# A two-layer trunk on one core: the attention gate in the output weights, the residual first in the accumulators, the overflow round behind the regular product

## The chip, the core and the metric

The kernel runs on one core of one Trainium2 chip. The metric is the device time of one execution in microseconds (us); the number for the kernel before is the median of 3 executions. The engines are TensorE (PE in the profile, its weight loads PEld), VectorE (DVE), ScalarE (ACT), GpSimd (POOL) and SyncE (SP), which here only issues transfers.

## The reference, cut to what matters

256 tokens of 1024 values pass through two layers, all in f32. Each is an attention, a residual with LayerNorm, a mixture of experts, and again a residual with LayerNorm.

```python
for l in range(2):
    sh_a, sc_a, g_a, sh_f, sc_f, g_f = split(silu(c) @ ada_w[l] + ada_b[l], 6)
    h = x * (1 + sc_a) + sh_a
    if l == 0:                     # 16 heads of 64, causal, with a forget gate
        q, k, v, f = h @ fox_w_in
        cum = cumsum(log_sigmoid(f + b_f))
        o = softmax(q k^T / 8 + cum_i - cum_j) v
    else:                          # 8 heads, two score maps each, value width 128
        k1, k2, v = (x * (1 + kv_sc) + kv_sh) @ kv_w
        q1, q2 = h @ diff_w_q
        o = (softmax(q1 k1^T / 8 + alibi) - lam * softmax(q2 k2^T / 8 + alibi)) v
        o = o * rsqrt(mean(o^2) + eps) * g * (1 - lam_init)
    x = layer_norm(alpha * x + (1 + g_a) * (o @ w_o))
    h = x * (1 + sc_f) + sh_f
    gates = grouped_top2(softmax(h @ router_w))      # 2 of 16 experts, from one of 4 groups
    m = sum(gates[e] * ((silu(h @ w_gate[e]) * (h @ w_up[e])) @ w_down[e]) for e in range(16))
    x = layer_norm(alpha * x + (1 + g_f) * m)
```

## The kernel before

**Weights.** 304 MB have to come from HBM. All large weights are cut into pieces of 2 MB, which pass through a ring of six slots. SP loads them in one fixed order; `spent` waits until the consumer of a slot has raised `used`, and `landed` makes a consumer wait for the transfer. A piece holds [1024, 512] of a weight (or [512, 1024] of a down weight).

**Modulation.** The 28 pieces of `ada_w` and `kv_ada_w` form seven groups of four, and not all are left to TensorE. For groups 1, 2, 5 and 6 VectorE multiplies the rows by their values of silu(c): `weigh` (L380 the first, L382 the seven others of a piece) sums the eight k slices of a piece into `acc`; `share(g, q)` is a quarter of a group, so one piece, `mod_sum(g)` lets TensorE add over the partitions (L1355), `mod_rows` adds the bias, `turn_mod` (L1389) turns shift and scale, `spread_gate` (L1397) with L863 spreads a gate row over the partitions into `gbc`. Group 4 goes through TensorE, as `mod_product(4)` (L1338), inside the route of layer 0.

**Layer 0's attention.** The stream is turned, scaled and shifted (`hT`). TensorE then projects keys, the forget gate's 16 columns (L1721, twice 8 columns for each of 8 k slices), values, and queries (`turned_units` L1430 and 1443, `natural_units` L1459). `forget_gate` on ScalarE (L679 to 681) and VectorE (L921 to 925) makes log-sigmoid and its running sum over 256 tokens. Then come 8 steps of one pair of heads each, with 3 more to drain the pipeline: scores, softmax (`soft`), probabilities out and turned (L1492), values, `fox_norm`, `pair_out`. TensorE puts one query unit in each step.

**Output and norm.** `out_part` (L1539) is the output projection, 64 products of 128x512 in layer 0 and 1 together, 32 each. `norm_sums` multiplies each half row block in PSUM by the gate (L992), adds alpha x (L993) and takes statistics (L995); `norm_stats` (L998) and GpSimd's `inv_std` (L548) finish them and L1006 normalises. `gained` on GpSimd (L555 multiply, L556 add, twice) makes the next residual x out of the normalised rows.

**Route.** `turn_stream` turns the normalised rows, `route` computes the router's logits, counts, and the position of each token for its expert; VectorE ranks (L1079 and after) and builds pick matrices (L1114, L1115); `gather` (L1597) fetches the tokens by product with them. `zeroed` (L1590) sets the four accumulator banks to zero with a product by zeros.

**Experts.** 16 experts are taken in 8 pairs. For expert j of a pair `gate_up` (L1615, L1616) makes gate and up for up to CAP = 64 tokens (GpSimd's L574 and L583 provide these windows), L1681 and L1688 turn them, `down` (L1626, L1627) follows, L1162 multiplies by the token's gate, and `add_back` (L1633) adds the 128 rows of a pair to the four accumulator banks by product with a put matrix; it runs one pair later. An expert with over 64 tokens has an `overflow` round: the same chain for the rest, with transposes L1650 and its own add-back. Here layer 0 has one such expert (10) and layer 1 two (11 and 14). The round of expert j stands ahead of expert j's regular product, and `gate_up` frees the two slots of j at its end. At the end of the layer `identa` (alpha on the diagonal) times x is added to the accumulators (L1703), then the last pair's add-back, and the second norm.

**Layer 1's attention.** Keys and values are shared projections of the stream, the query as before. It has 8 steps, one of one head with two score maps each; `diff_norm`, `head_out` and `heads_turned` follow, and output products (`out_part`) fill TensorE's places from step 4 on.

## Time and profile before

| | |
|---|---|
| runs of the kernel | 965.51, 965.51, 964.03 us; median 965.51 us |
| profiled execution | 970.29 us, span 968.6 us |
| mean granted TensorE clock | 0.965 |
| busy TensorE | 890.8 us (92%), 3754 instructions |
| busy weight load | 411.2 us (42%) |
| busy VectorE | 353.6 us (37%), 915 instructions |
| busy ScalarE | 170.6 us (18%) |
| busy GpSimd | 69.4 us (7%) |
| moved by DMA | 303.88 MB, mean 314 GB/s |

A busy share is the time in which an engine works on an instruction, over the span from the first to the last one. The weight load overlaps the products. The granted clock says at which of its two speeds TensorE was allowed to run: 1.0 is 2.4 GHz, 0.5 is 1.2 GHz. A matrix product's time is modelled from the trace, so a busy TensorE isn't necessarily one at its peak.

### The profile page before, as it was taken

To read this page: it belongs to the slowest core of one execution; us is meant where nothing else is said; L and a number is where in the kernel's file an instruction comes from. 1 tells how busy PE (TensorE), PEld (TensorE's weight loads), DVE (VectorE), ACT (ScalarE), POOL (GpSimd) and SP (SyncE) were. 2 spreads that over 40 slices of the span, in tenths; PEclk is the share of its full clock that TensorE was granted. 3 is DMA by queue.
4 is the path that set the end of the run, shared out by engine and by line. 5 is a ranking of instruction groups with operands and counts; after the bars stand their busy time and mean duration, and the time that the engine had idled before them with its cause. 6 is when DMAs were issued, how large, how long until landed. Compare 5 with 4: busy or idle time off the path is not lost.

```text
span 968.6 us, 11410 instructions
## 1 busy us (share of the span) xinstructions
PE 890.8 (92%) x3754; PEld 411.2 (42%) x3755; DVE 353.6 (37%) x915; ACT 170.6 (18%) x374; POOL 69.4 (7%) x110
## 2 busy tenths in 40 slices
PE   7899899999999897999989979889999989889895
PEld 3674674443333332233367458434333333233332
DVE  1286744472221122122259574347222212212215
ACT  1010242012111112011111025401211111111210
POOL 1000000003100000000040000200410000000000
PEclk9899999999999998699989989899999999999998
DMA  9999772848999999099984986212199999949901
GB/s 361 427 408 376 312 304 87 353 177 347 415 430 428 427 430 427 34 417 427 426 354 143 432 359 261 88 51 123 34 431 432 424 431 425 430 189 431 424 32 43
DMA packets 23360, 303.88 MB, mean 314 GB/s; under 512 B 2721, under 2 KB 3233, under 8 KB 5281
## 3 DMA queue, kind: packets, MB, share of 16 engines
q1 hardware_dynamic: 22752, 303.14, 75.2%
q8 instruction: 18, 0.29, 0.1%
q10 hardware_dynamic: 576, 0.34, 0.1%
q14 instruction: 14, 0.11, 0.0%
HBM read 302.42 MB, written 1.05 MB: 313 GB/s over the span
## 4 chain that ended last, share of the span: by engine, by line
PE 81%; DVE 9%; DMA 4%; issue 3%; ACT 1%; POOL 1%; SPq 0%; POOLq 0%; DVEq 0%; ACTq 0%
PE ps L1615 24%; PE ps L1626 12%; PE ps L1633 7%; PE ps L1430 6%; PE ps L1539 5%; PE ps L1443 4%; PE ps L1459 4%; DVE acc L382 3%; PE ps L1597 3%; DMA ring<-in_moe_w_up_dram 2%; DMA ring<-in_moe_w_down_dram 2%; PE ps L1362 1%; PE ps L1338 1%; PE ps L1590 1%; PE ps L1681 1%
## 5 line engine op out<-in xcount | busy, mean ns | idle before, releaser
L1615 PE MATMUL ps<-ring,hT 128*64 128x512 f32 x560 | 256.2, 609 | 17.5 <-issue 10.6
L1616 PE MATMUL ps<-ring,hT 128*64 128x512 f32 x560 | 256.6, 610 | 0.0
L1615 PEld LDWEIGHTS ps<-ring,hT 128*64 128x64 f32 x560 | 75.7, 140 | 177.3 <-issue 177.3
L1626 PE MATMUL ps<-ring,arena 128*64 128x512 f32 x280 | 130.4, 609 | 9.3 <-DMA ring<-in_moe_w_down_dram 5.9
L1627 PE MATMUL ps<-ring,arena 128*64 128x512 f32 x280 | 130.4, 609 | 0.0
L1153 DVE TENSOR_TENSOR arena<-arena,ps 128x256 f32<-128x256 f32 x32 | 13.5, 421 | 250.2 <-ACT arena L746 141.8
L382 DVE SCALAR_TENSOR_TENSOR acc<-ring,csig,acc 128x512 f32<-128x512 f32 x112 | 84.2, 752 | 4.0
L1616 PEld LDWEIGHTS ps<-ring,hT 128*64 128x64 f32 x560 | 75.7, 140 | 0.0
L1626 PEld LDWEIGHTS ps<-ring,arena 128*64 128x64 f32 x280 | 36.1, 139 | 77.4 <-issue 69.2
L1633 PE MATMUL ps<-arena 128*128 128x512 f32 x144 | 66.4, 604 | 0.0
L1162 DVE TENSOR_TENSOR arena<-ps,gbc 64x512 f32<-64x512 f32 x70 | 48.0, 686 | 48.1 <-PE ps L1627 47.0
L1430 PE MATMUL ps<-hT,ring 128*128 128x256 f32 x256 | 60.6, 402 | 3.0 <-ACT hT L631 3.0
L1430 PEld LDWEIGHTS ps<-hT,ring 128*128 128x128 f32 x256 | 51.9, 204 | 11.4 <-ACT hT L631 3.5
L1443 PE MATMUL ps<-ring,hT 128*128 128x512 f32 x128 | 55.8, 594 | 0.0
L583 POOL COPY hT<-arena 128x512 f32 x32 | 19.6, 615 | 432.3 <-PE ps L1616 341.2
L742 ACT ACTIVATE arena<-ps 128x512 f32<-128x512 f32 x16 | 9.6, 598 | 197.5 <-PE ps L1616 197.5
L1633 PEld LDWEIGHTS ps<-arena 128*128 128x128 f32 x144 | 26.0, 189 | 39.8 <-issue 39.8
L1443 PEld LDWEIGHTS ps<-ring,hT 128*128 128x128 f32 x128 | 24.2, 190 | 30.5 <-issue 30.4
L1627 PEld LDWEIGHTS ps<-ring,arena 128*64 128x64 f32 x280 | 36.1, 139 | 0.0
L1539 PE MATMUL ps<-ring,hT 128*128 128x512 f32 x64 | 30.6, 626 | 3.2 <-ACT hT L713 3.2
L1459 PE MATMUL ps<-h,ring 128*128 128x256 f32 x128 | 30.1, 389 | 0.5 <-ACT arena L673 0.5
L1459 PE MATMUL ps<-hT,ring 128*128 128x256 f32 x128 | 29.7, 385 | 0.5 <-ACT arena L673 0.5
(253 smaller groups left out, 905.2 us busy)
## 6 DMA issues: line engine op xcount, KB each, us to landing
ring<-in_moe_w_gate_dram SPq DMA_DIRECT2D x32, 2048.0 KB, 13.9
ring<-in_moe_w_up_dram SPq DMA_DIRECT2D x32, 2048.0 KB, 17.3
ring<-in_moe_w_down_dram SPq DMA_DIRECT2D x32, 2048.0 KB, 16.7
ring<-in_ada_w_dram SPq DMA_DIRECT2D x24, 2048.0 KB, 14.4
ring<-in_fox_w_in_dram SPq DMA_DIRECT2D x6, 2048.0 KB, 9.1
ring<-in_kv_ada_w_dram SPq DMA_DIRECT2D x4, 2048.0 KB, 12.1
ring<-in_kv_w_dram SPq DMA_DIRECT2D x4, 2048.0 KB, 20.5
ring<-in_fox_w_o_dram SPq DMA_DIRECT2D x2, 2048.0 KB, 13.2
```

The lines of the kernel that those rows point to most:

```text
L382: ins = alu.scalar_tensor_tensor(out=dst, in0=w[:, k, :], scalar=csig[:, k:k + 1], in1=dst, op0=ALU.mult, op1=ALU.add)
L1162: d.tensor_tensor(out[lo:lo + CAP, half], ps[part_, bank, :], gbc[part_, 1, half], ALU.mult).then_inc(done, 1)
L1430: mm = t.matmul(ps[:, u % 4, 0:S], wcols(piece)[:, k, cc * P:(cc + 1) * P], src[:, k, :], start=(k == 0), stop=(k == KC - 1))
L1443: mm = t.matmul(ps[:, u % 4, :], hT[:, k, b * P:(b + 1) * P], wcols(piece)[:, k, :], start=(k == 0), stop=(k == KC - 1))
L1459: mm = t.matmul(ps[:, 7, 0:S], wcols(n)[:, k, (c % 4) * P:(c % 4 + 1) * P], src[:, k, :], start=(k == 0), stop=(k == KC - 1))
L1539: mm = t.matmul(ps[:, 2 * b + s_, :], oT[l][:, k, b * P:(b + 1) * P], wcols(n)[:, k, :], start=(k == 0), stop=(k == KC - 1))
L1597: return t.matmul(ps[:, gather_bank(k), :], h[:, b, k * P:(k + 1) * P], pick[:, b, :], start=(b == 0), stop=(b == NB - 1))
L1615: mg = t.matmul(ps[0:CAP, bank, :], lhs(k), wcols(ng)[:, k, :], start=(k == 0), stop=(k == KC - 1))
L1616: mu = t.matmul(ps[CAP:P, bank, :], lhs(k), wcols(nu)[:, k, :], start=(k == 0), stop=(k == KC - 1))
L1626: t.matmul(ps[0:CAP, bank, :], lhs(f), wdown(n)[:, f, 0:512], start=(f == 0), stop=(f == 3))
L1627: mm = t.matmul(ps[CAP:P, bank, :], lhs(f), wdown(n)[:, f, 512:D], start=(f == 0), stop=(f == 3))
L1633: mm = t.matmul(ps[:, 2 * b + q, :], lhs(b), yy(q), start=False, stop=True, skip_group_check=True)
```

## The change

The gate `1 + g_a` of the attention is no longer applied to the product in PSUM: `gate_weights` multiplies the output weights' columns by it, in the ring's slots, on VectorE, during the steps of the attention, so `norm_sums` has one operation less in norms 0 and 2, and TensorE waits on `wo_r` where it waited on the transfer. Alpha x is put into the four banks during the route by `residual` (one block ahead of the counts, the other behind the gather), takes over the zeroing of the banks, and the add at the end of the layer goes; `gained` moves from behind the first pair to right behind the norm, block 1 first. In the expert loop the overflow round of expert j stands behind its regular product, on TensorE, ScalarE and VectorE. The slots of expert 0 are freed after one and two k slices of expert 1's product, those of expert 1 within the add-back.

The forget gate's product now goes four k slices side by side into four strips of 32 rows (`wf` has 32 columns per slice), and a second product with `fsum` adds the strips; that one stands behind the first two value units, and VectorE's part stands one unit later. The last quarter of group 2 is summed in steps 0 and 1 of layer 0's attention in place of ahead of them, and mod_sum(2) is issued in step 1; likewise the last quarter of group 6 in steps 0 to 2 of layer 1's attention, with mod_sum(6) behind query 3. In layer 1 `diff_norm(p - 1)` now stands ahead of `soft`. Of the route's filler, mod_product(4) takes the place of zeroing products in the norm and in the route, and turn_mod(4) moves up. The output products of layer 1 are regrouped around the turned heads. Some small tiles move from the arena into `fold`.

```diff
@@ -551,7 +556,7 @@
                 pool.wait_ge(xn_r, 4 * (norm + 1))
-                for b in range(NB):
+                for b in (1, 0):
@@ -593,12 +598,12 @@
                 pair(0, xs_ev)
-                gained(2 * l)
...
             number_slots(0)
+            gained(0)
@@ -675,7 +681,8 @@
             def forget_gate():
                 unit_filled(act, GATE_UNIT)
-                act.wait_ge(small_in, 16 * SMALL)
+                a.activation(fT, ps[:, 0, 0:S], ACT.Copy).then_inc(f_in, 1)
+                act.wait_ge(f_mm, 1)
@@ -740,10 +747,10 @@
                     a.activation(gu[:, 0, :], ps[:, 4, :], ACT.Copy).then_inc(gu_ev[0], 1)
-                    overflow(i, 1)
                     act.wait_ge(tg_mm[0], q + 1)
...
                     a.activation(sg[:, 0, :, :], gt[:, :, 0:CAP], ACT.Sigmoid).then_inc(sg_r[0], 1)
+                    overflow(i, 1)
                     spent(act, n0 + 3, i)
...
+            def gate_weights(l, s_, q):
+                n = N_WO[l][s_]
+                landed(dve, n)
+                w = wcols(n)[:, 4 * q:4 * q + 4, :]
+                d.tensor_tensor(w, w, gbc[:, 0, 512 * s_:512 * s_ + 512].unsqueeze(1).broadcast_to([P, 4, 512]),
+                                ALU.mult).then_inc(wo_r, 1)
             def diff_norm(hd):
@@ -989,9 +1010,8 @@
                     return
-                link(d.tensor_tensor(h[:, b, half], gbc[:, norm % 2, half], ps[:, 2 * b + s_, :], ALU.mult))
-                link(d.scalar_tensor_tensor(out=xres[:, b, half], in0=xres[:, b, half], scalar=ALPHA, in1=h[:, b, half],
-                                            op0=ALU.mult, op1=ALU.add))
+                link(d.scalar_tensor_tensor(out=xres[:, b, half], in0=xres[:, b, half], scalar=ALPHA,
+                                            in1=ps[:, 2 * b + s_, :], op0=ALU.mult, op1=ALU.add))
@@ -1195,8 +1215,8 @@
                     put_pair(i)
+                    glu(0, q)
                     overflow(i, 1)
-                    glu(0, q)
...
-                    forget_gate()
-                else:
+                if u != GATE_UNIT:
                     unit_out(u, dst, kind)
                 if u == GATE_UNIT + 1:
+                    forget_gate()
                     mod_rows(1)
@@ -1238,9 +1257,9 @@
             share(2, 2)
-            share(2, 3)
-            mod_rows(2)
             for p in range(PAIRS_H + 3):
+                if p == 2:
+                    mod_rows(2)
@@ -1251,10 +1270,16 @@
                     fox_norm(2 * p - 1)
+                if p < 2:
+                    share(2, 3, range(4 * p, 4 * p + 4))
                 if p >= 3:
                     pair_out(p - 3)
+                if p in (5, 6):
+                    gate_weights(0, 0, p - 5)
                 if p == PAIRS_H:
+                    gate_weights(0, 1, 0)
                     mod_rows(3)
+                    gate_weights(0, 1, 1)
             nothing_added()
@@ -1294,25 +1318,30 @@
                 slope = (2.0 ** (-8.0 * (p + 1) / HD))
-                if p == 1:
+                if p == 3:
                     mod_rows(6)
+                if 1 <= p < HD - 1:
+                    diff_norm(p - 1)
                 if p >= 2:
...
                     head_out(p - 4)
-                if p >= 1:
-                    diff_norm(p - 1)
+                if p < 3:
+                    share(6, 3, ((0, 1, 2), (3, 4, 5), (6, 7))[p])
+                elif p < HD - 1:
+                    gate_weights(1, (p - 3) // 2, (p - 3) % 2)
+            diff_norm(HD - 2)
             diff_norm(HD - 1)
             head_out(4)
-            heads_turned(1)
+            heads_turned(1, 7)
@@ -1401,8 +1430,10 @@
                 for b in range(NB):
-                    if b and norm != 1:
-                        zeroed((0, 1, 0, 1))
+                    if b and norm == 0:
+                        mod_product(4, range(0, 2))
+                    if b and norm == 2:
+                        zeroed((0, 1, 0))
...
+            def out_weights(l, count):
+                pe.wait_ge(wo_r, 4 * l + count)
             def scored(G):
...
             def route(l):
                 m = (1, 4)[l]
-                zeroed((2, 3))
+                if l == 0:
+                    mod_product(4, range(2, 4))
+                else:
+                    zeroed((0, 1))
...
                         k = 4 * kk + strip
-                        mm = t.matmul(ps[32 * strip:32 * strip + 32, 0, 0:S], rw[:, k, :], hT[:, k, :],
+                        mm = t.matmul(ps[32 * strip:32 * strip + 32, 2, 0:S], rw[:, k, :], hT[:, k, :],
@@ -1567,10 +1602,10 @@
                 if l == 0:
-                    zeroed((0, 2))
-                    mod_product(4, range(0, 4))
+                    mod_product(4, range(4, KC))
                 else:
-                    zeroed((0, 2, 3, 0, 2, 3))
+                    zeroed((0, 0, 0))
+                residual(l, 1)
@@ -1579,11 +1614,15 @@
                 if l == 0:
-                    mod_product(4, range(4, KC))
+                    turn_mod(4, 5)
                 pe.wait_ge(tot_r, l + 1)
-                zeroed((1,) if l == 0 else (1, 1, 1))
-                if l == 0:
-                    turn_mod(4, 5)
+                zeroed((1, 1, 1))
+            def residual(l, b):
+                pe.wait_ge(x_ready, 2 * NB * l + 2 - b)
+                for q in range(2):
+                    t.matmul(ps[:, 2 * b + q, :], identa[:, :], xres[:, b, q * 512:q * 512 + 512], start=True, stop=True)
@@ -1656,33 +1689,40 @@
                             pe.wait_ge(o_dve, k + 8)
-                            add_back(lambda bb: oputT[0:CAP, bb * P:(bb + 1) * P],
-                                     lambda q: oy[0:CAP, q * 512:q * 512 + 512]).then_inc(o_pe, 1)
+                            for bb in range(NB):
+                                for q in range(2):
+                                    mm = add_back(bb, q, oputT[0:CAP, :], oy[0:CAP, :])
+                            mm.then_inc(o_pe, 1)
                 gather()
+                residual(l, 0)
                 pe.wait_ge(tab, l + 1)
...
                     pe.wait_ge(tp_ev, q + 1)
-                    overflow(i, 0)
                     pe.wait_ge(y_ev[0], (q + 1) * 2)
...
                     pe.wait_ge(xw_r[0], q + 1)
-                    gate_up(0, i, lambda k: xw[:, 0, k, :], 4, range(KC), True)
+                    gate_up(0, lambda k: xw[:, 0, k, :], 4, range(KC))
+                    overflow(i, 0)
                     pe.wait_ge(y_ev[1], (q + 1) * 2)
-                    overflow(i, 1)
                     landed(pe, n0 + 2, i)
...
                     pe.wait_ge(xw_r[1], q + 1)
-                    gate_up(1, i, lambda k: xw[:, 1, k, :], 5, range(4), False)
+                    gate_up(1, lambda k: xw[:, 1, k, :], 5, (0,)).then_inc(used[slot(n0)], 1)
+                    gate_up(1, lambda k: xw[:, 1, k, :], 5, (1,)).then_inc(used[slot(n0 + 1)], 1)
+                    gate_up(1, lambda k: xw[:, 1, k, :], 5, range(2, 4))
                     pe.wait_ge(gu_ev[0], q + 1)
...
                     mm.then_inc(tg_mm[0], 1)
-                    gate_up(1, i, lambda k: xw[:, 1, k, :], 5, range(4, KC), True)
-                    add_back(lambda b: putT[:, b * P:(b + 1) * P],
-                             lambda qq: y[:, qq * 512:qq * 512 + 512]).then_inc(sc_mm, 1)
+                    gate_up(1, lambda k: xw[:, 1, k, :], 5, range(4, KC))
+                    overflow(i, 1)
+                    add_back(0, 0, putT, y).then_inc(used[slot(n0 + 2)], 1)
+                    add_back(0, 1, putT, y).then_inc(used[slot(n0 + 3)], 1)
+                    add_back(1, 0, putT, y)
+                    add_back(1, 1, putT, y).then_inc(sc_mm, 1)
                     pe.wait_ge(gu_ev[1], q + 1)
@@ -1697,17 +1737,12 @@
                     down(1, lambda f: aT[:, 1, f * CAP:(f + 1) * CAP], 5).then_inc(used[slot(n0 + 5)], 1)
-                pe.wait_ge(x_ready, 2 * NB * l + NB)
-                for b in range(NB):
-                    for q in range(2):
-                        t.matmul(ps[:, 2 * b + q, :], identa[:, :], xres[:, b, q * 512:q * 512 + 512],
-                                 start=False, stop=True, skip_group_check=True)
...
                 for b in range(NB):
-                    add_back(lambda b: putT[:, b * P:(b + 1) * P],
-                             lambda qq: y[:, qq * 512:qq * 512 + 512], (b,)).then_inc(sc_mm, 1)
+                    add_back(b, 0, putT, y)
+                    add_back(b, 1, putT, y).then_inc(sc_mm, 1)
@@ -1715,20 +1750,20 @@
             pe.wait_ge(small_in, 16 * SMALL)
-            for k in range(KC):
-                for half in range(2):
-                    lo = 64 * half
-                    mm = t.matmul(ps[lo:lo + PAIRS_H, 0, 0:S], wf[:, k, PAIRS_H * half:PAIRS_H * (half + 1)], hT[:, k, :],
-                                  start=(k == 0), stop=(k == KC - 1))
+            for kk in range(2):
+                for strip in range(4):
+                    mm = t.matmul(ps[32 * strip:32 * strip + 32, 0, 0:S], wf[:, 4 * kk + strip, :], hT[:, 4 * kk + strip, :],
+                                  start=(kk == 0), stop=(kk == 1))
...
             u = natural_units(u + 1, N_V[0][:1])
+            pe.wait_ge(f_in, 1)
+            t.matmul(ps[0:FROWS, 0, 0:S], fsum[:, :], fT, start=True, stop=True).then_inc(f_mm, 1)
...
             query_unit(0, 1, hT)
-            mod_sum(2)
@@ -1819,18 +1857,17 @@
             turn_heads(2)
+            turn_heads(3, 4)
+            spread_gate(3, 5)
...
                 out_part(1, 0, s_, range(4, 6))
-            turn_heads(3)
+            pe.wait_ge(ot_ev[1], 2)
             for s_ in range(2):
-                out_part(1, 1, s_, range(4, 6))
-            turn_mod(6, 4)
-            spread_gate(3, 5)
-            pe.wait_ge(ot_ev[1], 2)
-            for b in range(NB):
-                for s_ in range(2):
-                    out_part(1, b, s_, range(6, KC))
+                out_part(1, 0, s_, range(6, KC))
+            turn_mod(6, 7)
+            for s_ in range(2):
+                out_part(1, 1, s_, range(4, KC))
```

## Rows read from the trace of the kernel before

**Rows 1.** The page's slices: what the DMA queues moved, GB/s, 40 slices of 24.2 us.

```profile
GB/s 361 427 408 376 312 304 87 353 177 347 415 430 428 427 430 427 34 417 427 426 354 143 432 359 261 88 51 123 34 431 432 424 431 425 430 189 431 424 32 43
```

**Rows 2.** The chain of work that ended last: start, us on the chain, what.

```profile
368.11 18.66 DMA ring<-in_moe_w_down_dram
...
418.13 3.63 PE ps L1633 x8
...
482.10 3.63 PE ps L1703 x8
```

**Rows 3.** TensorE's timeline, expert stages: start, us, what, in brackets the wait before.

```profile
372.22 0.61 PE L1615 MATMUL ps<-ring,hT 128*64 128x512 f32 x1 [0.19 <-DMA ring<-in_moe_w_up_dram]
...
849.26 0.65 PE L1650 MATMUL ps<-ident,hT 128*128 128x128 f32 x4 [0.78 <-ACT hT L729]
...
857.02 3.70 PE L1633 MATMUL ps<-arena,fold 64*128 64x512 f32 x8 [1.51 <-DVE arena L1162]
```

**Rows 4.** Windows: length, busy PE, PEld, DVE, ACT, POOL, clock, DMA share, GB/s.

```profile
382.20:406.10 23.90, 17.77 (x38) 5.25 (x40) 2.78 (x8) 0.74 (x1) 0.00 (x0) 0.57 0.30 127
575.20:580.20 5.00, 4.95 (x20) 2.39 (x21) 2.05 (x11) 0.72 (x3) 0.00 (x0) 0.50 0.51 211
```

**Rows 5.** Timeline of layer 1's attention and its norm, TensorE and VectorE.

```profile
575.25 1.94 PE L1355 MATMUL ps<-acc,ones 128*32 128x512 f32 x8 [4.55 <-ACT arena L673]
...
614.11 5.47 PE L1539 MATMUL ps<-ring,hT 128*128 128x512 f32 x8 [2.36 <-ACT hT L713]
...
643.83 7.03 PE L1539 MATMUL ps<-ring,hT 128*128 128x512 f32 x16
...
657.43 0.21 DVE L998 BATCH_NORM_AGGREGATE mv<-bst 128x2 f32<-128x12 f32 x1
```

**Rows 6.** Timeline of layer 0's norm, route and gather.

```profile
181.87 13.90 PE L1539 MATMUL ps<-ring,acc 128*128 128x512 f32 x32
...
198.89 0.21 DVE L998 BATCH_NORM_AGGREGATE mv<-bst 128x2 f32<-128x12 f32 x1
...
200.18 1.15 DVE L1006 TENSOR_SCALAR h<-xres,mv,st 128x512 f32<-128x512 f32 x2 [1.08 <-POOL st L548]
...
207.42 0.19 DVE L1079 TENSOR_TENSOR rt<-rt,st 128x32 f32<-128x32 f32 x1
...
214.99 0.75 DVE L1115 SCALAR_TENSOR_TENSOR arena<-arena,ends 128x512 f32<-128x512 f32 x1
...
217.76 13.90 PE L1597 MATMUL ps<-arena,h 128*128 128x512 f32 x32
```

**Rows 7.** Timeline of layer 0's projections, gate and first scores.

```profile
65.59 3.63 PE L1721 MATMUL ps<-hT,wf 128*8 128x256 f32 x32
...
75.31 0.22 DVE L925 COPY arena<-arena 72x128 f32<-72x128 f32 x1
...
84.96 0.66 PE L1389 MATMUL ps<-ident,mrow 128*128 128x128 f32 x4 [0.81 <-DVE mrow L849]
...
110.85 1.06 PE L1355 MATMUL ps<-acc,ones 128*32 128x512 f32 x8 [2.13 <-DVE acc L382]
...
122.06 0.82 PE L1492 MATMUL ps<-ident,arena 128*128 128x128 f32 x6
```

**Rows 8.** VectorE's groups by line and shape: busy us, mean ns, idle before.

```profile
L382 DVE SCALAR_TENSOR_TENSOR acc<-ring,csig,acc 128x512 f32<-128x512 f32 x112 | 84.2, 752 | 4.0
L1162 DVE TENSOR_TENSOR arena<-ps,gbc 64x512 f32<-64x512 f32 x70 | 48.0, 686 | 48.1 <-PE ps L1627 47.0
L380 DVE TENSOR_SCALAR acc<-ring,csig 128x512 f32<-128x512 f32 x16 | 8.5, 534 | 0.1
L863 DVE SCALAR_TENSOR_TENSOR gbc<-ps,gbc 128x1024 f32<-128x1024 f32 x4 | 4.9, 1225 | 4.7 <-PE ps L1397 4.7
```

**Rows 9.** Timeline of VectorE and GpSimd, 502 to 506.

```profile
502.59 2.35 POOL L556 TENSOR_TENSOR xres<-xres,lnw 128x1024 f32<-128x1024 f32 x1
503.88 1.35 DVE L380 TENSOR_SCALAR acc<-ring,csig 128x512 f32<-128x512 f32 x1
```

106 lines of the change are left out of this document (56 added, 50 removed).

## The prediction

> **What bounds the kernel now.** I read the slices of the page first: the DMA row stands at 425 to 432 GB/s through most of the two expert stages, falls to 34 in the seventeenth slice (387 to 412 us) [rows 1]. Then the chain of work that ended last. In layer 0 it goes through a transfer of a down weight, from 368.11 on for 18.66 us, and reaches the add-back of the same pair at 418.13 only [rows 2]. The timeline places this: pair 5 (of 0 to 7) starts at 372.22 with expert 10's overflow round, which stands ahead of the regular product. Its gate and up product (16 half steps of 0.43) is over at 379.1, its transposes come about 1 us behind, and then TensorE waits for the weight until 386.8 [rows 3]. So transfers set the pace up to pair 5 (six pieces of 2.1 MB at 428 GB/s are 29.4 us, against some 26 us of products), and from there on TensorE does: gate and up slots 0 and 1 stay occupied through the overflow, the queue runs dry, TensorE waits, and its clock is 0.57 on average from 382 to 406 [rows 4].
>
> Outside the experts TensorE sets the time, with three kinds of gaps: sums of VectorE that it waits for (4.55 us at 575.25, 2.36 at 614.11) [rows 5], the norm behind the output products (last product ends at 195.8, statistics at 199.1; in layer 1 at 650.9 and 657.6) [rows 5, 6], and the clock after such gaps: 4.5 us of idleness around 572, then 5.0 us at 0.50, which is 1.2 GHz in place of 2.4 [rows 4, 5].
>
> **The change, part by part** (minus is time gained; the working is done on the profiled run of 970.29 us, whose span is 968.6; the median shown is 965.51).
>
> *Forget gate.* Its 16 products of 8 columns take 3.63 us at 65.59 [rows 7]; for four side by side I take a quarter and 0.2, 1.1, so the value product starts 2.5 us sooner. But the sum over strips is now issued behind the two value units (13.9 us) and everything of the gate stands behind it: it would run at 80.6 to 81.0. From the old product's end (69.2) to the gate's last copy (75.31 + 0.2) are 6.3 us of ScalarE and VectorE [rows 7]. VectorE does them ahead of mod_rows(1), so that copy is over at 81.0 + 6.3 + 0.7 = 88.0, and turn_mod, which ran at 84.96, waits 6 us on TensorE, with the gate rows and the other value units queued behind it, and on VectorE the sums of ada(2) wait behind the gate too: 3.15 later. Taken back: the 2.13 us wait for the last sum ahead of the scores and mod_sum(2) itself (1.06) no longer stand there, 3.2. Net 0. The clock: as after the gap at 572 [rows 4], 5 us at half, +2.5 (bounds 0 and 3.4).
>
> *share(2,3) in steps 0 and 1.* The moved half quarter is four operations of 0.75 to 0.79 us, 3.1 us [rows 8]. In step 1 it begins when VectorE has normalised, 9.3 us after the first scores; it is over 12.4 after them, mod_sum(2) needs it, and with its 1.06 us the transposes start 13.5 after them; now the first scores stand at 111.9 and those transposes at 122.06, 10.2 after them [rows 7]: +3.4 (bounds 0, if the half quarter fitted into VectorE's idle time, and 4.2). Later steps take 6.6 us of TensorE and leave VectorE 2.2 idle; into steps 5, 6 and 8 comes a gate product over 128x2048. By the row of 128x1024 (1.23 us) and that of 128x512 (0.69) one costs 2.3 us [rows 8] (bounds: 2.1 and four of the short ones, 2.8). The 0.1 to 0.2 it sticks out lies behind TensorE's 1.5 us between scores and values: 0. WO1 lands long before step 8.
>
> *Norm 0.* Four products of 0.69 go away. Only those of the last half count, because the last output product ends at 195.8: statistics at 195.8 + 0.2 + two operations 1.44 + 0.24 = 197.7, against 199.1: -1.4 [rows 6].
>
> *Route 0.* mod_product(4) replaces the zeroing products of equal length, and its second half (3.6 us) no longer stands between the counts and the gather, which starts at 217.76 though its first matrix was ready at 215.75: -1.9. The residual products (1.8 us each) fill places where zeroing or a wait stood: 0 while POOL is in time. That is where gained costs: four POOL operations, 2.42 us apart, now run right behind the norm, from 0.1 to 9.75 us after its end at 201.3, alongside VectorE's ranking, whose first operation on two SBUF tiles is at 207.42, 6.1 after it [rows 6]. The trace has one such meeting: L380, whose other 15 take 0.48 us on average (8.5 less 1.35, by 15) [rows 8], took 1.35 while POOL's L556 ran, and ended 0.3 behind it [rows 9]. The same here: L1079 waits for the third operation to end (7.3), L1080 for the fourth (9.75): +3.5 (0 if only L380's kind waits; 9.7 is the bound if each started later). TensorE then has 3.5 us with nothing, so I add 1.7 of clock. The Trainium skill, SBUF — State Buffer, section "SBUF: two separate sides", says that the shared ports are locked for a whole instruction, also against VectorE operations with two SBUF inputs. By that rule the sum stays as it is; without it both layers together would be 10.4 us shorter.
>
> *Experts.* Slots 0 and 1 are freed 0.9 and 1.7 us later, slots 2 and 3 the same. The transfers start that much later once: +0.9. After that four more pieces (19.6 us) are under way whenever slot 0 is freed, so nothing more. Pair 5 of layer 0: regular product 372.2 to 379.1, overflow product to 386.0, transposes at 387.0. A round not held by a transfer goes from transposes to add-back in 7.76 us (849.26 to 857.02) [rows 3]: add-back at 394.8, at full clock over at 398.4, then 7.5 us of expert 11's product, and the regular add-back at 405.9, against 418.13: -12.2. In layer 1 the rounds are expert 11's in pair 5 and one in pair 7; neither waits for its down weight, same work in another order: 0. Tail: 3.63 us of residual at 482.10 go; y needs two products of 0.69 [rows 8] and 0.2, so the last add-back can start at 483.7, not 485.7: -2.0, in each layer.
>
> *Attention 1.* The wait of 4.55 at 575.25 and the slow clock behind it [rows 4, 5] go, since 5.8 us of sums leave the place ahead of the first scores. Followed step by step (share of 2.1, 2.4 and 1.6 us in steps 0 to 2, mod_sum(6) once the query of step 3 is copied), the values of head 0 come 6 us sooner. Diff_norm ahead of soft ends a wait in step 7, 2 us more. VectorE's steps come to 6.0 us with the gate product against TensorE's 5.5 and slip 1.5 in all, so the first output product waits for the last gate product until 604.4, where it waits for the turned heads until 614.11 now: -9.7 so far [rows 5]. Behind it no slow stretch and four moved parts: the last output product ends at 638.2, not 650.9 (27.5 us of products, 32 of 0.86, and 6.3 of transposes, values and gate rows behind 604.4). The norm's first block now runs beside it, and the last statistics are out at 640.8, not 657.6: -16.8 in all. The transposes behind them lose their slow clock too (-1.1). POOL's lock and clock again: +3.5 and +1.7.
>
> Sum: layer 0: +2.5 + 3.4 - 1.4 - 1.9 + 3.5 + 1.7 + 0.9 - 12.2 - 2.0 = -5.5. Layer 1: -16.8 - 1.1 + 3.5 + 1.7 + 0.9 - 2.0 = -13.8. Together -19.3: 951.0 for the profiled run, 946.2 for the median.
>
> **Rivals.** *No lock*: POOL and VectorE pass each other. For it: one meeting is all the trace has, and L380 could have been late for another reason [rows 9]. -10.4 more: 935.8. *VectorE bounds attention 1*: its slips reach TensorE, or the gate product costs its upper bound of 2.8 and POOL's rms is late; half of the 16.8 is lost: 954.6. Against it: 2 us of slack per step now. *The overflow order brings nothing*: something other than the down weight ends that wait. Against it the chain's 18.66 us [rows 2]. 958.4. *Slower*: late slots starve the transfers. If each of the 14 pairs that follow a first one paid the 1.7 us, 24 us, the time would be 970; it turns from gain to loss at 1.4 us a pair. Against it: the queue holds four pieces then.
>
> **Chances.** Forecast 0.47 (its own range 941 to 951), no lock 0.25, VectorE-bound 0.15, overflow order without effect 0.08, starved transfers 0.05. The likeliest is 946; the range 934 to 957 takes in the second and third and leaves out less than 2 in 10. The measurement tells 0.2% (1.9 us) from no change. Faster 0.93, same 0.02, slower 0.05.
>
> **What would show it.** Turn_mod's products at about 88 with a 6 us gap before them and a clock of 0.5 behind it; 2 us of waiting at the moved mod_sum(2); L1079 and L1080 of up to 2.4 us under a POOL operation; no DMA slice under 100 GB/s in layer 0's experts, and pair 5's add-back about 34 us behind its start, where it is 46 now; first output product of layer 1 some 38 us behind the first scores, where it is 48 now. Wrong it would be if a transfer-bound pair took more than 29.4 us, or if the route took as long as before in spite of a waiting rank operation.

## The result, and the profile after

The changed kernel took 956.09 us (median of 6 executions), the kernel before 965.51: ratio 0.987, interval 0.984 to 0.990. Measured again, 955.33 against 967.08: 0.988 (0.984 to 0.992); one execution of the kernel before, 1063.07 us at a mean clock of 0.838, was in a slower state and isn't counted. The time is inside the range (934 to 957), one us below its upper end and 10 us above the forecast of 946: about half of the 19.3 us forecast. The profiled execution took 949.71, close to the 951.0 forecast for it, but it was the fastest of its kernel, and that of before (970.29) one of the slowest of its own. Between the two profiled ones 20.6 us are gone, between the medians 9 to 12.

The page's slices of the kernel after (TensorE's granted clock in tenths, and GB/s) answer to [rows 1]:

```profile
span 948.0 us, 11352 instructions
...
PE 869.6 (92%) x3720; PEld 404.5 (43%) x3721; DVE 370.2 (39%) x918; ACT 168.0 (18%) x373; POOL 69.7 (7%) x110
...
PEclk9999999998999999999989999998999999999998
...
GB/s 359 432 421 428 277 321 90 355 206 326 242 430 428 427 429 429 271 322 431 425 428 143 375 418 338 89 156 22 66 431 429 427 427 430 429 209 428 428 60 44
```

The seventeenth slice holds 271 GB/s in place of 34. The early stage, TensorE and VectorE, answers to [rows 7]:

```profile
62.71 1.07 PE L1755 MATMUL ps<-hT,wf 128*32 128x256 f32 x16
...
82.14 0.48 DVE L934 TENSOR_SCALAR fold<-ps,colb 72x256 f32<-72x256 f32 x1 [9.78 <-ACT fold L688]
...
85.09 1.12 PE L1418 MATMUL ps<-ident,mrow 128*128 128x128 f32 x4 [5.95 <-DVE mrow L862]
...
122.77 1.07 PE L1384 MATMUL ps<-acc,ones 128*32 128x512 f32 x8 [2.27 <-DVE acc L387]
```

Turn_mod's products stand behind a gap of 5.95 us and mod_sum(2) behind 2.27. The window behind the first gap (length, busy PE, PEld, DVE, ACT, POOL, clock, DMA share, GB/s) shows the clock at half for 3.4 us:

```profile
84.50:87.90 3.40, 2.81 (x7) 1.77 (x8) 3.26 (x6) 0.00 (x0) 0.00 (x0) 0.51 1.04 443
```

Layer 0's route, VectorE beside GpSimd, answers to [rows 6]:

```profile
206.21 2.37 POOL L560 TENSOR_TENSOR xres<-h,lnw 128x1024 f32<-128x1024 f32 x1
...
206.44 0.19 DVE L1095 TENSOR_TENSOR rt<-ps,st 128x32 f32<-128x32 f32 x1
206.93 0.19 DVE L1097 TENSOR_REDUCE st<-rt 128x2 f32<-128x32 f32 x1 [0.29 <-ACT rt L725]
207.15 0.17 DVE L1098 RECIPROCAL st<-st 128x2 f32<-128x2 f32 x1
207.35 1.27 DVE L1099 TENSOR_TENSOR rt<-rt,st 128x32 f32<-128x32 f32 x1
208.66 2.42 POOL L561 TENSOR_TENSOR xres<-xres,lnw 128x1024 f32<-128x1024 f32 x1
208.66 0.19 DVE L1100 TENSOR_TENSOR rt<-rt,rb 128x32 f32<-128x32 f32 x1
208.89 2.34 DVE L1072 TENSOR_TENSOR rc<-rt 128x128 f32<-128x128 f32 x1
...
214.80 0.64 PE L1612 MATMUL ps<-rt,before 128*128 128x32 f32 x2 [3.14 <-DVE rt L1111]
```

L1099 (0.19 us in the kernel before) takes 1.27 and ends with GpSimd's operation; the next, L1100, still takes 0.19, and its record begins at the same 208.66 as that of GpSimd's fourth operation; L1072 (0.29 alone) takes 2.34. L1095, which reads PSUM, is not held, nor are L1097 and L1098, which read one SBUF tile each. TensorE waits 3.14 us for the ranks, 4.13 in layer 1, and behind both waits its clock is at half for 6.8 us (layer 0 here: 206 to 226):

```profile
206.00:216.00 10.00, 6.86 (x44) 2.89 (x43) 8.38 (x26) 0.83 (x2) 5.00 (x3) 0.91 0.51 185
216.00:226.00 10.00, 10.00 (x24) 5.13 (x24) 6.51 (x29) 0.00 (x0) 0.00 (x0) 0.75 1.01 429
```

Pair 5 of layer 0, the tail, and layer 1's attention, on TensorE, answer to [rows 2, 3, 5]:

```profile
392.97 0.65 PE L1683 MATMUL ps<-ident,hT 128*128 128x128 f32 x4 [0.78 <-ACT hT L736]
395.57 1.11 PE L1662 MATMUL ps<-ring,fold 128*64 128x512 f32 x1 [1.72 <-DVE fold L1205]
402.16 3.70 PE L1667 MATMUL ps<-arena,fold 64*128 64x512 f32 x8 [1.51 <-DVE arena L1182]
413.54 3.70 PE L1667 MATMUL ps<-arena 128*128 128x512 f32 x8
...
479.84 3.67 PE L1667 MATMUL ps<-arena 128*128 128x512 f32 x8 [1.60 <-DVE arena L1182]
...
575.64 1.06 PE L1384 MATMUL ps<-acc,ones 128*32 128x512 f32 x8 [0.56 <-ACT arena L679]
...
599.09 3.70 PE L1572 MATMUL ps<-ring,hT 128*128 128x512 f32 x8 [1.19 <-DVE ring L986]
...
625.93 7.03 PE L1572 MATMUL ps<-ring,hT 128*128 128x512 f32 x16
```

The 5.88 us wait for the down weight is gone, pair 5 (start 378.29) reaches its add-back 35.3 us later, and 45.8 before. Mod_sum(6) waits 0.56 in place of 4.55, and the last output product ends at 633.0, not 650.9. VectorE's groups (busy us, mean ns | idle before):

```profile
L986 DVE TENSOR_TENSOR ring<-ring,gbc 128x2048 f32<-128x2048 f32 x8 | 18.3, 2283 | 0.0
...
L1072 DVE TENSOR_TENSOR rc<-rt 128x128 f32<-128x128 f32 x2 | 4.7, 2330 | 0.1
L1099 DVE TENSOR_TENSOR rt<-rt,st 128x32 f32<-128x32 f32 x2 | 2.5, 1234 | 0.1
```

### The profile page after: what moved, and what is told of

It is laid out like the page before. It is cut to its first block, busy times and chain, and to the rows that moved or that the text cites. A ratio compares the mean times of both kernels' runs of the same rounds, so it can differ in the third digit from the quotient of the medians.

```text
span 948.0 us, 11352 instructions
## 1 busy us (share of the span) xinstructions
PE 869.6 (92%) x3720; PEld 404.5 (43%) x3721; DVE 370.2 (39%) x918; ACT 168.0 (18%) x373; POOL 69.7 (7%) x110
## 4 chain that ended last, share of the span: by engine, by line
PE 79%; DMA 9%; DVE 7%; issue 2%; ACT 1%; POOL 0%; SPq 0%; DVEq 0%; ACTq 0%
PE ps L1654 23%; PE ps L1662 10%; DMA ring<-in_moe_w_up_dram 8%; PE ps L1667 7%; PE ps L1461 6%; PE ps L1474 6%; PE ps L1490 6%; PE ps L1572 5%; PE ps L1636 3%; PE ps L1718 1%; PE ps L1629 1%; PE ps L1391 1%; DMA ring<-in_ada_w_dram 1%; PE ps L1523 1%; PE ps L1426 1%
## 5 line engine op out<-in xcount | busy, mean ns | idle before, releaser
L1654 PE MATMUL ps<-ring,hT 128*64 128x512 f32 x560 | 251.4, 600 | 17.7 <-DMA ring<-in_moe_w_up_dram 9.3
L1655 PE MATMUL ps<-ring,hT 128*64 128x512 f32 x560 | 251.8, 601 | 0.0
L1663 PE MATMUL ps<-ring,arena 128*64 128x512 f32 x256 | 116.7, 599 | 0.0
L1662 PE MATMUL ps<-ring,arena 128*64 128x512 f32 x256 | 116.7, 598 | 0.0
L1173 DVE TENSOR_TENSOR arena<-arena,ps 128x256 f32<-128x256 f32 x32 | 13.5, 421 | 240.8 <-ACT arena L752 132.1
L1461 PE MATMUL ps<-hT,ring 128*128 128x256 f32 x256 | 58.3, 392 | 3.4 <-issue 1.9
L1662 PEld LDWEIGHTS ps<-ring,arena 128*64 128x64 f32 x256 | 32.4, 136 | 60.1 <-issue 60.1
L1474 PE MATMUL ps<-ring,hT 128*128 128x512 f32 x128 | 55.8, 594 | 0.0
L1474 PEld LDWEIGHTS ps<-ring,hT 128*128 128x128 f32 x128 | 24.2, 190 | 30.5 <-issue 30.4
L1663 PEld LDWEIGHTS ps<-ring,arena 128*64 128x64 f32 x256 | 32.4, 136 | 0.0
L1490 PE MATMUL ps<-hT,ring 128*128 128x256 f32 x128 | 29.7, 385 | 0.5 <-ACT arena L679 0.5
L1572 PE MATMUL ps<-ring,hT 128*128 128x512 f32 x64 | 28.6, 594 | 1.2 <-DVE ring L986 1.2
## 6 DMA issues: line engine op xcount, KB each, us to landing
ring<-in_kv_w_dram SPq DMA_DIRECT2D x4, 2048.0 KB, 19.3
```

What stands on the lines that cost most here:

```text
L1461: mm = t.matmul(ps[:, u % 4, 0:S], wcols(piece)[:, k, cc * P:(cc + 1) * P], src[:, k, :], start=(k == 0), stop=(k == KC - 1))
L1474: mm = t.matmul(ps[:, u % 4, :], hT[:, k, b * P:(b + 1) * P], wcols(piece)[:, k, :], start=(k == 0), stop=(k == KC - 1))
L1490: mm = t.matmul(ps[:, 7, 0:S], wcols(n)[:, k, (c % 4) * P:(c % 4 + 1) * P], src[:, k, :], start=(k == 0), stop=(k == KC - 1))
L1572: mm = t.matmul(ps[:, 2 * b + s_, :], oT[l][:, k, b * P:(b + 1) * P], wcols(n)[:, k, :], start=(k == 0), stop=(k == KC - 1))
L1654: t.matmul(ps[0:CAP, bank, :], lhs(k), wcols(ng)[:, k, :], start=(k == 0), stop=(k == KC - 1))
L1655: mm = t.matmul(ps[CAP:P, bank, :], lhs(k), wcols(nu)[:, k, :], start=(k == 0), stop=(k == KC - 1))
```

## The experiments

Executions of one kernel differ by 2 to 12 us, so each row of this table has, beside the median time, the mean over its executions of span and of granted clock, and the mean of span times clock of each: the span with each us at half clock counted half. "Of before" is the ratio with its interval. The changed kernel stands twice, as first measured and again. The rows were measured at three times, and the kernel before, each time beside them, had medians of 967.1, 968.8 and 968.1 us and 937.6, 937.9 and 939.0 in span times clock: a difference of 1 to 2 us between two rows of the table says little.

| kernel | median us | of before | span | clock | span x clock |
|---|---|---|---|---|---|
| before_again | 968.28 | 1.000 (0.997 to 1.003) | 965.1 | 0.971 | 937.3 |
| before_order | 962.91 | 0.996 (0.994 to 0.999) | 960.9 | 0.975 | 936.7 |
| changed | 956.09 | 0.987 (0.984 to 0.990) | 953.6 | 0.971 | 926.2 |
| again | 955.33 | 0.988 (0.984 to 0.992) | 953.6 | 0.970 | 925.0 |
| old_order | 954.01 | 0.986 (0.982 to 0.989) | 951.8 | 0.973 | 926.3 |
| sum2_first | 953.99 | 0.987 (0.983 to 0.991) | 951.3 | 0.970 | 922.8 |
| sum6_first | 962.12 | 0.994 (0.992 to 0.997) | 960.1 | 0.967 | 928.8 |
| gate_in_norm | 958.11 | 0.991 (0.988 to 0.994) | 956.6 | 0.972 | 929.9 |
| late_x | 950.97 | 0.982 (0.979 to 0.986) | 948.5 | 0.975 | 924.9 |
| gate_later | 946.40 | 0.978 (0.973 to 0.983) | 943.9 | 0.976 | 921.1 |
| fix_both | 939.48 | 0.972 (0.968 to 0.976) | 937.9 | 0.982 | 921.0 |
| fix_old | 938.14 | 0.972 (0.968 to 0.977) | 937.6 | 0.984 | 922.9 |
| fix_three | 936.94 | 0.969 (0.965 to 0.973) | 935.1 | 0.983 | 918.8 |

**Both kernels again.** No edit. For the changed one and the one before:

> The changed kernel unaltered, to see how its executions differ. Its six executions lay between 949.71 and 958.81 us with a mean granted clock of 0.978 down to 0.968, and the profiled one was the fastest. Theory: they do the same work and differ only in how many stretches TensorE runs at 1.2 GHz, so span times clock stays constant (948.0 x 0.978 = 927, 956.9 x 0.968 = 926), and a slower execution shows more half-clock stretches in its records, none at the places that the change made busy. Median 953 to 958, ratio 0.987 to 0.992. Rival: executions differ in waits for transfers; span times clock would then spread by several us, and the TensorE waits in the expert stages would be longer in a slower one.

> The kernel before unaltered. The profiled execution was 970.29 us at clock 0.965 (968.6 x 0.965 = 935), its others had a median of 965.51. By the theory of one constant product, 965.5 goes with a clock of 0.970, and the change is worth 8 to 9 us at equal clock and not the 20.6 between the two profiled executions. Rival: at equal clock the difference is 17 us or more, the clock of before is then 0.975 or more at 965 us. Ratio to before 0.998 to 1.002.

Measured: the first holds. Over the changed kernel's twelve executions the span runs from 948.0 to 956.9 and the clock from 0.978 to 0.966, but span times clock only from 923.0 to 927.1. Before and changed have the same mean clock (0.971 and 0.970 to 0.971) and differ by 11 to 12 us in span times clock, so the gain is work and waits, and none of it clock. My figure of 8 to 9 us at equal clock came from two single executions and was too low; the rival's 17 falls.

**old_order.** In the changed kernel, on TensorE (ScalarE and VectorE likewise):

```diff
                     pe.wait_ge(tp_ev, q + 1)
+                    overflow(i, 0)
                     pe.wait_ge(y_ev[0], (q + 1) * 2)
...
-                    gate_up(0, lambda k: xw[:, 0, k, :], 4, range(KC))
-                    overflow(i, 0)
+                    gate_up(0, lambda k: xw[:, 0, k, :], 4, range(KC), True)
                     pe.wait_ge(y_ev[1], (q + 1) * 2)
+                    overflow(i, 1)
```

> The changed kernel with the overflow rounds ahead of the regular products again, and the gate and up slots freed at the end of their product. The forecast's term: the order was worth 12.2 us in layer 0 against 0.9 for late slots in each layer, so this comes out 10.4 slower than the changed kernel, about 966. The two traces gave 9.2 between pair 5's start and its add-back, so by them +9, and TensorE waits 5 to 6 us for expert 10's down weight again with no transfer from its gate product to pair 6. Rival (the order brings nothing): within 2 us of the changed kernel.

Measured: 954.01 against 955.33, not 9 to 10 slower. The rival holds for the time, though not for the reason that the prediction gave it: the wait for the down weight is back. TensorE's timeline of old_order, and the window over pair 5 up to pair 6, then that of the kernel after and that of before:

```profile
392.94 1.12 PE L1665 MATMUL ps<-ring,fold 128*64 128x512 f32 x1 [5.87 <-DMA ring<-in_moe_w_down_dram]
```

```profile
378.36:430.06 51.70, 43.55 (x176) 15.47 (x178) 9.19 (x23) 8.07 (x10) 1.23 (x2) 0.93 0.68 284
```

```profile
378.20:425.00 46.80, 42.78 (x178) 14.88 (x176) 9.34 (x23) 8.07 (x10) 1.23 (x2) 0.96 0.71 296
```

```profile
372.20:429.60 57.40, 49.23 (x178) 16.77 (x180) 9.21 (x23) 8.08 (x10) 1.23 (x2) 0.82 0.61 256
```

With the same wait the place takes 51.7 us at clock 0.93 and 57.4 at 0.82. Of the 10.6 us between before and after, 5.7 were the clock behind the wait and 4.9 the order, and the order gives 2.0 back: in old_order's and again's traces 138.75 and 140.72 us lie between pair 0's and pair 5's start, as the slots come free later. Before_order, the same edit the other way, has 139.43 where both traces of before have 138.74, and fix_both further down has 139.48 where fix_old has 139.82, so this price is between nothing and 2.0. These are single traces, each with its own stretches at half clock: from pair 5 of layer 1 to the last statistics old_order takes 135.0 us at a clock of 0.95 and again 129.1 at 1.00, and with the corrections it is the other way round (fix_old 129.5, fix_both 133.8).

**before_order.** The kernel before, with the changed kernel's order and slot releases in the expert loop:

```diff
-                    overflow(i, 0)
                     pe.wait_ge(y_ev[0], (q + 1) * 2)
...
-                    gate_up(0, i, lambda k: xw[:, 0, k, :], 4, range(KC), True)
+                    gate_up(0, i, lambda k: xw[:, 0, k, :], 4, range(KC), False)
+                    overflow(i, 0)
                     pe.wait_ge(y_ev[1], (q + 1) * 2)
-                    overflow(i, 1)
...
-                    gate_up(1, i, lambda k: xw[:, 1, k, :], 5, range(4), False)
+                    gate_up(1, i, lambda k: xw[:, 1, k, :], 5, (0,), False).then_inc(used[slot(n0)], 1)
+                    gate_up(1, i, lambda k: xw[:, 1, k, :], 5, (1,), False).then_inc(used[slot(n0 + 1)], 1)
+                    gate_up(1, i, lambda k: xw[:, 1, k, :], 5, range(2, 4), False)
```

> The kernel before with one part of the change: the overflow rounds behind the regular products on TensorE, ScalarE and VectorE, with the slot releases that this needs. Undoing it in the changed kernel cost nothing measurable. New theory: the order saves about 3 us of work in pair 5 of layer 0 and nothing in layer 1, the later slots cost 2 us in each layer before pair 5, and what was large in the trace of before was the slow clock behind the 5.9 us wait (20.4 us at half, 10.2 lost), which isn't there in each execution. So span times clock stays within 2 of before's 937, the time is 0 to 5 us shorter, by as much as the slow stretch in pair 5 goes. The forecast's term of 12.2 less 1.8 asks for 10.4 us shorter, 957.

Measured: 5.9 us faster than the 968.78 beside it (by mean spans 4.6), span times clock the same within 1, clock 0.975 for 0.971. So in this kernel the order is worth some 5 us (the interval allows 1 to 6), all of it clock; in the changed one it is worth nothing that the runs tell (old_order's clock is not lower). Neither is the forecast's 10.4.

**late_x.** Gained behind the route's tables, both residual blocks behind the gather, zero products in the first one's place:

```diff
             number_slots(0)
+            pool.wait_ge(tab, 1)
             gained(0)
...
-                residual(l, 1)
+                zeroed((3, 3, 3, 3))
                 pe.wait_ge(rt_mask, l + 1)
...
                 gather()
+                residual(l, 1)
                 residual(l, 0)
```

> The changed kernel with gained behind VectorE's route tables (GpSimd waits for them) and both residual blocks behind the gather; zero products stand where the first residual block stood. Theory of the port: no VectorE operation of the ranking takes 1.2 or 2.3 us, the counts come 3.1 to 3.5 sooner, TensorE's gap of 3.1 and 4.1 us and the slow clock behind it (1.7) go, and 1.9 us of residual stand behind the gather, partly over the wait for the windows of the first pair: 3 to 5 us a layer, 6 to 9 in all, about 948. Rival (the gap has another cause, or a 1.2 GHz stretch only moves elsewhere): under 3 us in all.

Measured: 4.4 us faster, between the 6 to 9 expected and the rival's "under 3". In span times clock nothing is gained (924.9, again 925.0): the gain is clock. Its timeline of VectorE, GpSimd and TensorE (the two ranking operations are now L1101 and L1074):

```profile
212.66 0.19 DVE L1101 TENSOR_TENSOR rt<-rt,st 128x32 f32<-128x32 f32 x1
213.11 0.29 DVE L1074 TENSOR_TENSOR rc<-rt 128x128 f32<-128x128 f32 x1
...
218.53 0.30 PE L1614 MATMUL ps<-rt,before 128*128 128x32 f32 x2
...
226.51 2.35 POOL L560 TENSOR_TENSOR xres<-h,lnw 128x1024 f32<-128x1024 f32 x1 [20.68 <-DVE tabb L1157]
226.66 2.22 DVE L887 TENSOR_TENSOR modc<-colb 128x8 f32<-128x8 f32 x1
...
236.32 3.60 PE L1627 MATMUL ps<-xres,identa 128*128 128x512 f32 x8
```

Both run at 0.19 and 0.29, TensorE's wait is gone, and the lock has moved with GpSimd to an operation off the path (L887, 2.22 in place of 0.17; it holds up the scaling of the first gathered rows, not of the last). From the last output product to the gather 19.9 us pass in place of 23.25 (again), and 19.6 in place of 25.4 in layer 1, less 1.6 in each for the residual behind the gather: 1.8 and 4.2, 6.0 in these traces. Two things changed together: the ranks come 3.1 us sooner behind the logits, and the zero products fill 1.7 us more than the residual block did (3.7 for 2.0), so that in layer 0 TensorE reaches the counts 1.6 us after the ranks are out (216.93). The 6.8 us at half clock are gone in both layers. Whether a shorter filler would do as well no run shows.

**gate_later.** In VectorE's projections:

```diff
                 if u == GATE_UNIT + 1:
-                    forget_gate()
                     mod_rows(1)
...
                     share(2, 0)
+                    forget_gate()
```

> The changed kernel with VectorE's part of the forget gate moved behind mod_rows(1) and the first quarter of ada(2). Theory: turn_mod waits for VectorE's gate work only, so its 5.95 us gap falls to under 2 and the slow stretch behind it goes; VectorE itself gains only the 3 us that it waited for ScalarE's logarithm, so its last sum comes 3 us sooner and TensorE then waits about 5 at mod_sum(2) where it waits 2.3: 3 us shorter, up to 5 if the clock stays high, 950 to 953. Rival (something else, a transfer, ends the gap): no change.

Measured: 946.40, 8.9 us faster than the changed kernel, more than expected. Its TensorE timeline:

```profile
81.55 0.66 PE L1418 MATMUL ps<-ident,mrow 128*128 128x128 f32 x4 [0.81 <-DVE mrow L862]
...
117.89 1.07 PE L1384 MATMUL ps<-acc,ones 128*32 128x512 f32 x8 [2.28 <-DVE acc L387]
```

The gap is 0.81, and the wait at mod_sum(2) didn't grow; it is 2.28, as in again. My reckoning that the 5 us would turn up there was wrong: VectorE starts the last half quarter when it has done a softmax, so those sums follow TensorE's scores and come earlier with them (mod_sum(2) stands 12.65 us behind the first scores in both). In span times clock it is 4 to 5 us, the rest is clock (0.976). The executions spread from 939.0 to 950.6, so the 8.9 is good to some 4 us.

**sum6_first, sum2_first.** The moved quarters undone, one each, with mod_sum and mod_rows of that group where they stood before:

```diff
             share(6, 2)
+            share(6, 3)
...
-                if p < 3:
-                    share(6, 3, ((0, 1, 2), (3, 4, 5), (6, 7))[p])
```

```diff
             share(2, 2)
+            share(2, 3)
+            mod_rows(2)
             for p in range(PAIRS_H + 3):
...
-                if p < 2:
-                    share(2, 3, range(4 * p, 4 * p + 4))
```

> The changed kernel with the last quarter of group 6 summed ahead of layer 1's first scores again and mod_sum(6) ahead of step 1, as before. The forecast gave 16.8 us to attention 1 and its norm, with this move as the start of it. Theory: the 4 to 5 us wait at mod_sum(6) and 3 us of slow clock come back, the following steps run without the 6.1 us of sums: 5 to 7 us slower in all, 960 to 962. Rival (VectorE bounds the whole phase, wherever the sums stand): under 2 us slower.

> The changed kernel with the last quarter of group 2 summed ahead of the first scores and mod_sum(2) there, as before. The forecast said that moving it costs 3.4 us net of 3.2 taken back. Theory: the 2.3 us wait at mod_sum(2) and its 1.1 us leave step 2, but VectorE's 6.1 us of sums stand ahead of the first scores, where VectorE idles only 7.6 us until its first softmax: TensorE waits there for the last sum by 0 to 3 us. Within 2 us of the changed kernel, 953 to 957. If VectorE's time ahead of the scores were free, 3 us faster.

Measured: 962.12 and 953.99. Their waits at mod_sum, on TensorE:

```profile
572.98 1.94 PE L1383 MATMUL ps<-acc,ones 128*32 128x512 f32 x8 [4.29 <-ACT arena L679]
```

```profile
112.64 1.06 PE L1382 MATMUL ps<-acc,ones 128*32 128x512 f32 x8 [0.57 <-ACT arena L679]
```

In layer 1 the move is worth 6.8 us, 3 in span times clock and the rest clock. In layer 0 it is worth nothing (1.3 us the other way, 2 to 3 in span times clock): there VectorE was in time for the first scores, and the move made the wait. It was in time because TensorE had already lost 5.95 us at turn_mod; in the kernel before, TensorE waited 2.13 us for the same sum [rows 7]. What the place of these sums is worth beside gate_later no run shows.

**gate_in_norm.** No gate_weights (TensorE waits for the transfers of the output weights again), the gate in `norm_sums` again:

```diff
-                link(d.scalar_tensor_tensor(out=xres[:, b, half], in0=xres[:, b, half], scalar=ALPHA,
-                                            in1=ps[:, 2 * b + s_, :], op0=ALU.mult, op1=ALU.add))
+                link(d.tensor_tensor(h[:, b, half], gbc[:, 0, half], ps[:, 2 * b + s_, :], ALU.mult))
+                link(d.scalar_tensor_tensor(out=xres[:, b, half], in0=xres[:, b, half], scalar=ALPHA, in1=h[:, b, half],
+                                            op0=ALU.mult, op1=ALU.add))
```

> The changed kernel with the gate in the norm again (one more product of 0.69 us per half block in norms 0 and 2) and none of the eight products over 128x2048 on the output weights. Forecast: 1.4 us longer at each of the two norms; the 1.2 us for which layer 1's first output product waits for the last weight product go, and step times of VectorE fall. Theory: 1 to 2 us slower, 956 to 958. Rival (the weight products hold up the attention steps by more than they save): as fast or faster.

Measured: 958.11, 2.8 slower than again (4 to 5 in span times clock). The statistics of norm 0 come 3.3 us behind the last output product, in the changed kernel 1.7 (199.03 less 197.33). So the 18.3 us of weight products that VectorE took on (L986) do lie beside other work, all but the 1.2 us for which layer 1's first output product waits for the last of them.

**The corrections together.** Fix_both is late_x and gate_later; fix_old adds old_order; fix_three adds to fix_both, on TensorE (VectorE's mod_rows(2) likewise; mod_sum(2) stands at the head of the loop's step 2 in the changed kernel, not in step 1 as the text on the change has it):

```diff
-                if p == 2:
+                if p == 3:
                     mod_sum(2)
```

> The changed kernel with both corrections, gained behind the route's tables (4.4 us faster alone) and VectorE's gate work later (8.9 alone). They lie in different stages. If each is a saving of work plus a slow stretch of its own, they add: 13 less, 942. If part of each was luck of the granted clock, they add in span times clock (925 less 4 to 5) and the time lands at 943 to 947.

> fix_both, and mod_sum(2) one step of heads later still (step 3 in place of 2), where VectorE's last sum has long been done. Theory: TensorE's wait of 2.3 us ahead of it goes and nothing else waits for group 2 until the modulation of the route: 2.3 less than fix_both, up to 4 with the clock. Rival (VectorE is then late at the next softmax instead, since it has the same sums to do): the wait moves to the next transposes and the time stays within 1.

> fix_both with the overflow rounds ahead of the regular products again. Undone alone it changed the time by -1.3 (span times clock +1), so the same is expected here: within 3 us of fix_both, 3 longer if the 5.9 us wait brings 20 us of slow clock as in the two profiles of the kernel before, 0 if 7 as in old_order's profile.

Measured: 939.48, 936.94 and 938.14. The two do more than add in time (4.4 and 8.9 make 13.3, measured 15.9), below both ranges expected. In span times clock fix_both stands where gate_later stands alone (921.0 and 921.1), so what late_x brings is clock again (0.982). In fix_three the wait of 2.28 is 0.56:

```profile
123.03 1.07 PE L1386 MATMUL ps<-acc,ones 128*32 128x512 f32 x8 [0.56 <-ACT arena L681]
```

and 2.5 us are gone, 2.2 in span times clock, so the rival falls. The order again makes no difference in time (-1.3; by span times clock fix_old does 1.9 more). Fix_three is the fastest: 3% less than the kernel before, 2% less than the changed one.

## Why the prediction was right, and what in it was wrong

The direction and the range held; of the 19.3 us forecast 9 to 12 came.

*Forget gate.* The mechanism was right: turn_mod at 85.1 (forecast 88) behind a gap of 5.95 (6), half clock behind it for 3.4 us (5). From the gate's product to the first scores 46.3 us passed in both traces of before and 47.4 and 48.1 in those of the changed kernel, 1.1 to 1.8 more, clock included, for the +2.5 forecast. (The first scores came 1.7 us earlier in the profiled execution, 110.12 for 111.85, only because the gate's product did, by 2.9: 30 to 50 us, which lie ahead of the first changed product, ran at 0.83 in before and at 1.00 in this one. In again's trace it is 0.83 too.)

```profile
30.00:50.00 20.00, 17.67 (x81) 14.04 (x74) 7.33 (x18) 1.86 (x4) 0.00 (x0) 0.83 1.01 432
30.00:50.00 20.00, 17.68 (x94) 14.56 (x87) 8.69 (x20) 1.86 (x4) 0.00 (x0) 1.00 1.00 428
```

It was not weighed that the place of one call on VectorE made all of it; moved, it gives back 8.9 us, more than the term's +2.5.

*share(2,3).* A wait of 2.27 (2 forecast) at the place named, and the first transposes 13.65 us behind the first scores (13.5). Of the +3.4 the forecast took back 3.2 in the term before, so the move was to cost 0.2; sum2_first shows 1 to 3.

*Norm 0.* -1.4 forecast, -1.6 by gate_in_norm's trace; the weight product 2.28 us, 2.3 forecast.

*Route.* L1079 (now L1099) was held as foreseen; the second was L1072, not L1080, which got through as one GpSimd operation gave way to the next. TensorE's wait was 3.14 and 4.13 for 3.5 each. Half clock followed in both layers for 6.8 us, which costs up to 3.4 each and not 1.7. The rival *no lock* falls. The Trainium skill, SBUF — State Buffer, section "SBUF: two separate sides", says that VectorE and GpSimd share ports that are locked for a whole instruction; L1099, L1072 and L887 agree, and so does L1095, which reads PSUM and was not held. Late_x, net of its own residual products, gave 4.4 us for both layers, all of it clock; the forecast had 10.4 gross.

*Experts.* This is the step that failed, the term "-12.2" for the overflow order. Its mechanism was seen (no wait for the weight, no slice under 100 GB/s, 35.3 us from pair 5's start to its add-back, about 34 forecast), but its size was that of one execution with the clock at half for 20.4 us in pair 5. Put into the kernel before, the order is worth 5.9 us, and in the changed kernel nothing (old_order, fix_old). The late slots cost between nothing and 2.0 in layer 0, where 0.9 was forecast. The tail was right: 13.3 us from the last add-back but one to the last, 15.1 before, for -2.0. Two rivals give times nearer the measured 956.09 than the forecast's 946: "VectorE bounds attention 1" (954.6), which the trace refutes, and "the overflow order brings nothing" (958.4, chance 0.08), whose reason is refuted and whose effect comes near what the changed kernel shows.

*Attention 1.* Right: the first output product 38 us behind the first scores (561 to 599.09), last statistics 22.2 us earlier, of which 5.7 come from layer 0, so 16.5 for 16.8; again's trace against before_again's gives 16.5 too. It is the largest real gain, and sum6_first shows 6.8 of it to be the moved quarter. Of the rest gate_in_norm shows 2.3 (this stage takes 150.8 us in its trace, 148.5 in again's); diff_norm ahead of soft and the regrouped output products were never undone alone, so their share is not shown. "VectorE bounds attention 1" falls, and so do starved transfers.

*The sum.* The starts of each norm's last statistics (L998, now L1018) cut a trace into stages:

```profile
492.48 0.21 DVE L998 BATCH_NORM_AGGREGATE mv<-bst 128x2 f32<-128x12 f32 x1
962.67 0.21 DVE L998 BATCH_NORM_AGGREGATE mv<-bst 128x2 f32<-128x12 f32 x1
```

```profile
198.82 0.21 DVE L1018 BATCH_NORM_AGGREGATE mv<-bst 128x2 f32<-128x12 f32 x1
486.83 0.21 DVE L1018 BATCH_NORM_AGGREGATE mv<-bst 128x2 f32<-128x12 f32 x1
635.23 0.21 DVE L1018 BATCH_NORM_AGGREGATE mv<-bst 128x2 f32<-128x12 f32 x1
942.13 0.21 DVE L1018 BATCH_NORM_AGGREGATE mv<-bst 128x2 f32<-128x12 f32 x1
```

| us | up to norm 0 | route and experts 0 | attention 1 | route and experts 1 |
|---|---|---|---|---|
| forecast | +4.5 | -10.0 | -16.8 | +3.0 |
| before to changed, the profiled pair | -0.1 | -5.6 | -16.5 | +1.7 |
| before_again to again | +6.5 | -6.4 | -16.5 | +1.8 |

The forecast for the profiled pair (951.0 for 949.71) was met by luck: the first stage came out 4.6 us too good, mostly by the clock of one execution, and the second 4.4 us too poor. The first of these is absent in the second pair, the miss in the experts is in both. I took the slow stretches of one execution of before as a cost that the change removes, and put 4.8 us on account of the difference to the median. The mean clock did not rise: 0.971 before and after. What remains is 11 to 12 us of span times clock, less than attention 1 alone gives.

**Open:** why the clock stays low for long in one execution and not in another at the same wait. Gate_later, late_x and both together, which took waits of TensorE away, raised the mean clock (0.970 to 0.976, 0.975 and 0.982), but sum2_first, which takes one of 2.3 us away, did not (0.970), and old_order, which brings a 5.87 us wait back, did not lower it.

## What to carry to other kernels

Gain read off one profiled execution holds slow-clock stretches that others lack: compare span times granted clock over several executions, and book what a stall costs in clock apart from the stall. When a product is moved to spare TensorE time, look at what its result's consumer blocks on its own in-order engine: here one call moved behind two others on VectorE was worth 8.9 us, nearly as much as the whole change. Long GpSimd operations on SBUF belong beside VectorE work that nothing waits for.

## What the runs showed of the hardware that was not expected

A VectorE operation on two SBUF tiles that meets a 2.4 us GpSimd operation doesn't wait for the whole train of them: it ends with the one under way (1.27 and 2.34 us), and L1100, 0.19 us long on two SBUF tiles, got through where one GpSimd operation ended and the next began. Operations with one SBUF input, a reduction and a reciprocal, kept their 0.19 and 0.17 us. And the clock behind one and the same wait of 5.9 us was at half for 20.4 us in both profiles of the kernel before and for 6.8 in old_order's (and in fix_old's, around a wait of 4.57 us).
